# Attention's step regrouped, and the mLSTM in pairs of heads, in a hybrid layer's inference step

## The chip, the cores and the metric

The kernel runs on one core of one Trainium2 chip. The metric is the device time of one execution in microseconds; the number for a kernel is the median of its runs. PE is TensorE, DVE is VectorE, ACT is ScalarE, POOL is GpSimd, SP is the engine that issues most DMAs. Everything is fp32.

## The reference, cut to what matters

One inference step of a two-layer encoder for a prompt of 2048 tokens and a sample of 64 tokens with a past of 1024. Layer 0 projects its input into two parallel mixers, whose results are gated, joined and projected. Layer 1 is a gated DeltaNet and is not touched here. The first mixer is attention over 8 heads (96 wide for scores, 64 wide for values), causal in chunks of 64:

```python
s = einsum('bqhd,bkhd->bhqk', q, k) * (q.shape[-1] ** -0.5)
p = softmax(where(mask, s, -inf), axis=-1)
o = einsum('bhqk,bkhd->bqhd', p, v)
```

The second is the mLSTM over 4 heads (64 wide for q and k, 128 wide for v), with a state C, a normaliser n and a running maximum m:

```python
sqk = einsum('bhlk,bhsk->bhls', q, k) * exp(dmat - m[..., None])
num = w_inter[..., None] * einsum('bhlk,bhkv->bhlv', q, C0) + einsum('bhls,bhsv->bhlv', sqk, v)
den = w_inter * einsum('bhlk,bhk->bhl', q, n0) + sum(sqk, axis=-1)
h   = num / maximum(abs(den), exp(-m))[..., None]
C1  = decay_end[..., None, None] * C0 + einsum('bhl,bhlk,bhlv->bhkv', wk, k, v)
n1  = decay_end[..., None] * n0 + einsum('bhl,bhlk->bhk', wk, k)
```

## The kernel before, in words

The program is a chain of phases: `setup`, `project_a`, `attend`, `mlstm`, `project_c`, `local`, `recur`. Each phase ends with all engines meeting. Inside a phase every engine has its own stream, written by hand, and the streams meet by semaphores.

**`attend`.** The order of tiles is the sample tile (64 queries, 1088 keys: 9 key tiles, the last of 64) and then prompt tiles 0 to 15 of 128 queries; prompt tile t has t + 1 key tiles of 128. A step `s` is one head of one tile, 8 x 17 = 136 steps and 5 to drain. PE's loop (end of its block) does in step s: `scores(s)` (L974, one matmul per 512 keys), then the work of older heads: `turn(s - 1, g)` (L987) transposes the probabilities of the head before, in groups of up to 4 key tiles, and `values(p, js)` (L1009) multiplies transposed probabilities by v for a pair of older heads, one head into PSUM partitions 0 to 63 and the other into 64 to 127, in turn. Half of the pair's key tiles are done in each step. Before the change they are cut into as many portions as there are groups, and a portion follows each group of transposes. An fp32 matmul leaves two records in the trace, a transpose one.

The scores stand in PSUM (`ps`, 16 key tiles wide). A tile of more than 8 key tiles has two pieces (halves of `ps`), so the scores of a piece wait (`before_at`) until the exp of the same piece of the head before has read it. A tile of up to 8 has one piece, and heads alternate between the halves. DVE adds the diagonal mask (L1185), takes the row maximum of each piece (L1191, L1188, L1195), and then copies those transposed groups whose running number is even (`copies(s - 1, 0)`, L1075) out of the two PSUM buffers `pst`. ACT does the exp (L1109, one ACTIVATE and an accumulator read for each piece) and copies the odd groups (L1082): before the change the first of its copies goes ahead of the exp of piece 0 and the second ahead of the exp of piece 1. The transposes of a group wait for the copy of the group two before it. Once in a tile, at step 8k + 12, PE transposes the finished output back (L1021), DVE divides and gates it (L1205 to L1215), and POOL stores it (L949).

Between these, `gates(s)` does the mLSTM's gate sums and exponents, and POOL sets the initial mLSTM state at the start: a memset, and three DMAs for the sample's maximum, C and n.

**`mlstm`.** 17 tiles (16 prompt tiles, then the sample). Per tile, PE runs `numerators(t)` (for each of the 4 heads: L1430, intra: sq by v, 128 rows; and at once L1431, inter: qwT by C, 64 rows, into the same PSUM), `updates(t)` (L1441, kw by v, into PSUM partitions 0 to 63 of the banks CA and CB), `maxima(t + 1)` (L1378), `scores(t + 1)` (L1387, 64 rows), `turn_qk(t + 2)` (L1369), `turn_qw(t + 1)` (L1395), then the output projection of the tile before (`project`, L1415, 16 matmuls of 512 columns), and `turn_mix(t)` (L1406). ACT's `split_heads` (L1472, L1473) copies the transposed q, k and qw, which come with two heads on 128 partitions, into tiles of 64 partitions for all heads. DVE's `heads`, `mask`, `gated`, `state` (L1591, L1595), `weigh` (L1543) and `residual` follow. `BANK` and `order` name the PSUM bank of each product and the order in which a bank's products follow each other. SP loads q, k, v two to three tiles ahead and stores the two states at the end (`store_state`, 3 DMAs each).

Of the kernel before, what the change touches and what calls it, by code (L numbers as in the profile page):

```python
# [777 lines left out]
def attend(nc, io, sc, K):  # L778


    with ExitStack() as ctx:
# [142 lines left out]
        def _(pool):  # L924
# [29 lines left out]
            pool.wait_ge(m_init_in, 48)  # L954

        @block.tensor
        def _(pe):
# [90 lines left out]
            for s in STEPS:  # L1048
# [31 lines left out]
        def _(act):  # L1080
# [13 lines left out]
            for s in STEPS:  # L1094
                gates(s)
                mine = copies(s - 1, 1) if 1 <= s <= N else []
                for i in range(2):
                    if i < len(mine):
                        copy_turned(act, copy, s - 1, mine[i])
                    if s < N and i < pieces[head(s)[0]]:  # L1100
                        t, h = head(s)
                        n = rows(t)
                        if i == 0:
                            act.wait_ge(row_max, s + 1)
                            if s >= 2:
# [5 lines left out]
                                             accum_out=sums[at(t) % 2][:n, h, i:i + 1]).then_inc(expd, 1)  # L1111
                k = (s - 11) // H
# [8 lines left out]
        def _(dve):  # L1121
# [3 lines left out]
            def gates(s):  # L1125
# [20 lines left out]
                if s == 26:  # L1146
# [10 lines left out]
                    dve.wait_ge(m_init_in, 48)  # L1157
# [60 lines left out]
def mlstm(nc, io, sc, K):  # L1218


    with ExitStack() as ctx:
# [3 lines left out]
        def sem(name):  # L1225
# [17 lines left out]
        qT = sb("qT", [MK, MH, P])  # L1243
        kT = sb("kT", [MK, MH, P])
        qwT = sb("qwT", [MK, MH, P])
# [13 lines left out]
        x1_stored = [sem(f"x1_stored{u}") for u in range(2)]  # L1259
        qkv_in = [sem(f"qkv_in{u}") for u in range(RING)]  # L1260
# [4 lines left out]
        BANK = {"numA": 0, "qwT": 0, "numB": 1, "mixT0": 1, "CA": 2, "CB": 3, "y0": 4, "turn": 5, "y1": 5, "D": 6, "mixT1": 6,  # L1265
                "qk": 7}
        order = [(n, 0) for n in ("turn", "qk", "D")] + [("turn", 1), ("qwT", 0)]
        for t in range(TILES + 1):
            now, behind, ahead = t < TILES, t > 0, t + 1 < TILES
            order += [(n, t) for n in ("numA", "numB", "CA", "CB") if now]  # L1270
            order += [(n, t + 1) for n in ("D", "qk") if ahead]
# [30 lines left out]

        block = ctx.enter_context(nc.Block())

        @block.sync
        def _(sp):
# [12 lines left out]
            def store_state(s):  # L1319
                pre, last = "ps"[s], (NT - 1, TS)[s]  # L1320
                for name in ("CA", "CB"):
                    used(sp, name, last)
# [1705 lines left out]
```

## Time and profile before

| | us |
|---|---|
| median of 3 runs | 3954.46 (3951.67 to 3955.92) |
| the profiled execution's own time | 3945.66 |
| its span, first to last instruction | 3944.1 |
| PE busy | 3713.9, 94% of the span, mean granted clock 0.958 |
| PE's weight loads / DVE / ACT / POOL busy | 2163.4 / 1693.4 / 1090.2 / 402.7 |
| PE busy in `attend`'s scores, transposes, values (L974, L987, L1009) | 303.6, 197.9, 203.6 |
| PE busy in `mlstm`'s projection (L1415) | 236.5 |

The busy time of PE is the union of matmuls that overlap, and the end of each is modelled; times from one start to the next are the better measure of what a matmul costs. Most of the kernel's time lies in phases that the change doesn't touch. The profiled execution is one of the faster ones, so its span is a little below the median.

### The profile page before, as it was taken

Reading aid. Unit: us, or ns where it says so; the run is one execution under the profiler, and the core shown is the slowest. Engines: PE = TensorE matmul, PEld = TensorE weight load, DVE = VectorE, ACT = ScalarE, POOL = GpSimd, SP = SyncE. Lnnn points to the kernel's source line nnn. Section 1 sums busy time; section 2 is a strip of 40 time slices with the busy share of each in tenths; the row PEclk is TensorE's granted clock in tenths of the full one; section 3 lists DMA queues with packets and bytes.
Section 4 is the critical chain, followed back from the end, with each engine's and each line's share of the span. In section 5 each row is a group of like instructions: output and inputs, shape, how many; then the busy total and the mean of one; then the engine's idle time right before and its main releaser. Section 6 shows DMA issues by size and latency. Waiting matters only on the chain. (4 is left out here: it accounts for less than half of the span.)

```text
span 3944.1 us, 46043 instructions
## 1 busy us (share of the span) xinstructions
PE 3713.9 (94%) x17237; PEld 2163.4 (55%) x17237; DVE 1693.4 (43%) x2959; ACT 1090.2 (28%) x2809; POOL 402.7 (10%) x553
## 2 busy tenths in 40 slices
PE   7899999999979999998999499999999989699998
PEld 3455555555445555665555355555555558666665
DVE  2122222222235555554544244344443447477784
ACT  0211121121124444432211223233232236322222
POOL 0000000000000000000000010000000001343451
PEclk9899999999959999998999699999999998799999
DMA  5712221221073000004321611111111129855652
GB/s 179 241 60 63 78 66 53 75 72 58 28 180 77 25 23 19 11 9 142 107 86 59 221 43 47 53 60 55 44 59 39 55 82 259 235 156 157 173 146 80
DMA packets 349425, 362.15 MB, mean 92 GB/s; under 512 B 129539, under 2 KB 277742, under 8 KB 347054
## 3 DMA queue, kind: packets, MB, share of 16 engines
q1 hardware_dynamic: 307238, 305.44, 26.1%
q10 hardware_dynamic: 35112, 30.37, 2.5%
q0 software_dynamic: 6880, 23.73, 2.1%
q8 instruction: 124, 2.03, 0.2%
q14 instruction: 71, 0.58, 0.0%
HBM read 231.45 MB, written 128.01 MB: 91 GB/s over the span
## 5 line engine op out<-in xcount | busy, mean ns | idle before, releaser
L523 PE MATMUL a_bank<-a_w_in,a_hT 128*128 128x512 f32 (+4 forms) x1904 | 754.1, 554 | 2.2 <-ACT a_hT L612 2.2
L1849 PE MATMUL d_bank<-d_hT,d_w_in 128*128 128x512 f32 (+1 forms) x1920 | 724.0, 534 | 8.1 <-DMA d_w_in<-in_c_w_in 4.5
L523 PEld LDWEIGHTS a_bank<-a_w_in,a_hT 128*128 128x128 f32 (+1 forms) x1904 | 351.5, 187 | 367.5 <-issue 316.6
L1849 PEld LDWEIGHTS d_bank<-d_hT,d_w_in 128*128 128x128 f32 x1920 | 339.7, 195 | 351.1 <-issue 338.2
L974 PE MATMUL c_ps<-c_kT,c_q 96*128 96x512 f32 (+5 forms) x688 | 303.6, 576 | 23.2 <-DMA c_kT<-scratch_kT 15.9
L2670 PE MATMUL r_bank<-k_w_next,r_mixT 128*128 128x512 f32 (+1 forms) x544 | 250.3, 610 | 2.1 <-ACT r_mixT L2728 2.1
L1855 PE MATMUL d_bank<-d_w_in,d_hT 128*128 128x344 f32 (+3 forms) x816 | 245.2, 455 | 0.0
L1982 DVE SCALAR_TENSOR_TENSOR d_cv<-d_xb,k_wconv,d_cv 128x512 f32<-128x512 f32 (+1 forms) x360 | 236.9, 658 | 12.8
L1415 PE MATMUL m_bank<-m_w_out,m_mixT 128*128 128x512 f32 (+1 forms) x544 | 236.5, 593 | 0.7 <-ACT m_mixT L1499 0.7
L1980 DVE TENSOR_SCALAR d_cv<-d_xb,k_wconv 128x512 f32<-128x512 f32 (+1 forms) x120 | 52.9, 441 | 396.7 <-ACT d_xb L1922 389.3
L1191 DVE TENSOR_REDUCE c_part<-c_ps 128x1 f32<-128x1024 f32 (+9 forms) x144 | 137.6, 960 | 178.9 <-PE c_ps L974 176.5
L974 PEld LDWEIGHTS c_ps<-c_kT,c_q 96*128 96x128 f32 (+1 forms) x688 | 124.0, 197 | 158.0 <-issue 133.1
L987 PE MATMUL c_pst<-k_consts,c_prob 128*128 128x128 f32 (+1 forms) x1160 | 197.9, 287 | 13.1 <-ACT c_prob L1109 7.4
L1009 PE MATMUL c_pso<-c_probT,c_v 128*64 128x128 f32 (+1 forms) x2320 | 203.6, 291 | 0.2 <-DVE c_probT L1075 0.2
L1109 ACT ACTIVATE c_prob<-c_ps,c_negmax 128x1024 f32<-128x1024 f32 (+8 forms) x208 | 176.9, 852 | 81.1 <-DVE c_negmax L1195 43.1
L1855 PEld LDWEIGHTS d_bank<-d_w_in,d_hT 128*128 128x128 f32 (+1 forms) x816 | 149.8, 187 | 81.2 <-issue 11.3
L1082 ACT ACTIVATE c_probT<-c_pst 128x512 f32<-128x512 f32 (+3 forms) x172 | 94.2, 547 | 313.3 <-PE c_pst L987 313.0
L987 PEld LDWEIGHTS c_pst<-k_consts,c_prob 128*128 128x128 f32 (+1 forms) x1160 | 132.4, 145 | 81.0 <-issue 46.8
L1415 PEld LDWEIGHTS m_bank<-m_w_out,m_mixT 128*128 128x128 f32 (+1 forms) x544 | 100.3, 187 | 124.6 <-issue 124.5
L2670 PEld LDWEIGHTS r_bank<-k_w_next,r_mixT 128*128 128x128 f32 (+1 forms) x544 | 99.3, 189 | 116.7 <-issue 112.2
L1925 ACT ACTIVATE d_xb<-d_cv 128x512 f32<-128x512 f32 (+1 forms) x120 | 66.6, 555 | 337.0 <-DVE d_cv L1982 337.0
L1922 ACT ACTIVATE d_xb<-d_bank 128x512 f32<-128x512 f32 (+1 forms) x120 | 62.7, 522 | 343.2 <-PE d_bank L1849 335.6
(364 smaller groups left out, 4408.1 us busy)
## 6 DMA issues: line engine op xcount, KB each, us to landing
k_n_kv<-scratch_qkv SPq DMA_DIRECT2D x17, 1024.0 KB, 5.3
scratch_qkv<-d_ts SPq DMA_DIRECT2D x64, 256.0 KB, 2.3
a_w_ada<-in_c_w_ada SPq DMA_DIRECT2D x16, 768.0 KB
d_w_in<-in_c_w_in ACTq DMA_DIRECT2D x6, 2048.0 KB, 21.3
l_kT<-scratch_g_kT SPq DMA_DIRECT2D x17, 512.0 KB, 5.4
l_qT<-scratch_g_qT SPq DMA_DIRECT2D x17, 512.0 KB, 5.7
k_n_kT<-scratch_g_kT SPq DMA_DIRECT2D x17, 512.0 KB, 5.8
r_qT<-scratch_g_qT SPq DMA_DIRECT2D x17, 512.0 KB, 8.3
```

Of the source, the lines that this page charges most:

```text
L523: mm = nc.tensor.matmul(o[:n, 0:w], hT[u][:, k, :n], w_in[:, k, c0:c0 + w], start=(k == 0), stop=(k == KD - 1))
L974: mm = nc.tensor.matmul(ps[:n, o:o + b - a], q[k % 2][:, h, :n], kT[:, h, col0[t] + a:col0[t] + b], start=True, stop=True)
L987: mm = nc.tensor.transpose(pst[c % 2][:w, j % 4, :n], prob[s % 2][:n, j * P:j * P + w], ident[:n, :n])
L1009: mm = nc.tensor.matmul(pso[k % 2][u * DV:(u + 1) * DV, h0 // 2, :n], v[:w, col0[t] // P + j, (h0 + u) * DV:(h0 + u + 1) * DV], probT[(2 * ...
L1082: return nc.scalar.activation(out, src, ACT.Copy)
L1109: nc.scalar.activation(prob[s % 2][:n, c0:c1], ps[:n, o:o + c1 - c0], ACT.Exp, bias=negmax[:n, s % 2:s % 2 + 1], accum_out=sums[at(t) % 2] ...
L1191: nc.vector.tensor_reduce(part[:n, s % 2, i:i + 1], ps[:n, o:o + c1 - c0], AXX, ALU.max).then_inc(part_max, 1)
L1415: mm = nc.tensor.matmul(o[:n, :], mixT[:, k, :n], w_out[:, k, half * 512:(half + 1) * 512], start=(k == 0), stop=(k == KD - 1))
L1849: mm = nc.tensor.matmul(o[:, 0:w.w], w_in[:, k, w.a * P:(w.a + 1) * P], hT[w.r % 2][:, k, 0:w.w], start=(k == 0), stop=(k == KD - 1))
L1855: mm = nc.tensor.matmul(o[:n, 0:c1 - c0], hT[w.r % 2][:, k, w.a * P:w.a * P + n], w_in[:, k, GC + c0:GC + c1], start=(k == 0), stop=(k == ...
L1982: ins = nc.vector.scalar_tensor_tensor(cv[:, 0:w.w], xb[u][:, j:j + w.w], tap[j], cv[:, 0:w.w], ALU.mult, ALU.add)
L2670: mm = nc.tensor.matmul(o[:n, :], mixT[:, k, :n], w_out[:, k, half * 512:(half + 1) * 512], start=(k == 0), stop=(k == KD - 1))
```

## The change

In `attend`, PE does the first two groups of transposes, then all of the step's values, and then the remaining groups. ACT makes its copy of group 0 or 1 ahead of the exps and those of groups 2 and 3 behind both exps.

In `mlstm`, heads 2a and 2a + 1 lie at partitions 0 to 63 and 64 to 127 of one tile (`place(h)`): q, k, qw and the states C. PSUM banks hold even heads (`num0`, `qk0`) and odd heads (`num1`, `qk1`). The numerators are done as four intra products and then four inter products, the inter ones alternating between the two partition halves; the next tile's scores move ahead of the updates and alternate too; the updates write both PSUM halves of one bank. ACT's copies and DVE's state additions are merged over the 128 partitions, DVE's weigh and decay are split in two. The initial state takes 5 DMAs on POOL in place of 3, the stores of the states 10 on SP in place of 6. The diff, cut to its core:

```diff
@@ attend, gpsimd
-                pool.dma_start(K["m_C1"][:, :, 0:MV], io["state_mlstm_C"].rearrange("h k v -> k h v")).then_inc(m_init_in, 16)
-                pool.dma_start(K["m_C1"][:, :, MV:], io["state_mlstm_n"].rearrange("h k -> k h").unsqueeze(2)).then_inc(m_init_in, 16)
+                for b in range(2):
+                    half = slice(b * MK, (b + 1) * MK)
+                    pool.dma_start(K["m_C1"][half, :, 0:MV], io["state_mlstm_C"].rearrange("(a b) k v -> b k a v", b=2)[b]).then_inc(m_init_in, 16)
+                    pool.dma_start(K["m_C1"][half, :, MV:], io["state_mlstm_n"].rearrange("(a b) k -> b k a", b=2)[b].unsqueeze(2)).then_inc(m_init_in, 16)
@@ attend, tensor
-                    for g in range(n_g):
+                    for g in range(min(2, n_g)):
                         turn(e, g)
-                        values(p, js[g * len(js) // n_g:(g + 1) * len(js) // n_g])
+                    if js:
+                        values(p, js)
+                    for g in range(2, n_g):
+                        turn(e, g)
@@ attend, scalar
+                if mine and mine[0] < 2:
+                    copy_turned(act, copy, s - 1, mine[0])
                 for i in range(2):
-                    if i < len(mine):
-                        copy_turned(act, copy, s - 1, mine[i])
...
+                for g in mine:
+                    if g >= 2:
+                        copy_turned(act, copy, s - 1, g)
@@ mlstm
-        BANK = {"numA": 0, "qwT": 0, "numB": 1, "mixT0": 1, "CA": 2, "CB": 3, "y0": 4, "turn": 5, "y1": 5, "D": 6, "mixT1": 6,
-                "qk": 7}
+        BANK = {"num0": 0, "qwT": 0, "num1": 1, "mixT0": 1, "C": 2, "qk1": 3, "y0": 4, "turn": 5, "y1": 5, "D": 6, "mixT1": 6,
+                "qk0": 7}
+        def place(h):
+            return slice(h % 2 * MK, h % 2 * MK + MK), h // 2
@@ mlstm, tensor: scores
+                banks = [claim(pe, f"qk{b}", t) for b in range(2)]
                 used(pe, "turn", t)
                 for h in range(MH):
-                    mm = nc.tensor.matmul(o[:n, h * P:h * P + n], kT[:, h, :n], qT[:, h, :n], start=True, stop=True)
+                    (half, a), (o, fill) = place(h), banks[h % 2]
+                    mm = nc.tensor.matmul(o[:n, a * P:a * P + n], kT[half, a, :n], qT[half, a, :n], start=True, stop=True)
@@ mlstm, tensor: numerators
-                for half, name in enumerate(("numA", "numB")):
-                    o, fill = claim(pe, name, t)
-                    for h in range(2):
-                        c = slice(h * (MV + 1), (h + 1) * (MV + 1))
-                        nc.tensor.matmul(o[:n, c], sq[:n, 2 * half + h, :n], vx[u][:n, 2 * half + h, :], start=True, stop=False)
-                        mm = nc.tensor.matmul(o[:n, c], qwT[:, 2 * half + h, :n], C[s][:, 2 * half + h, :], start=False, stop=True)
-                    mm.then_inc(fill, 1)
+                for h in range(MH):
+                    a, o = h // 2, banks[h % 2][0]
+                    mm = nc.tensor.matmul(o[:n, a * (MV + 1):(a + 1) * (MV + 1)], sq[:n, h, :n], vx[u][:n, h, :],
+                                          start=(a == 0), stop=False)
...
+                used(pe, "qwT", t)
+                if 0 < t < TS:
+                    used(pe, "C", t - 1)
+                for h in range(MH):
+                    (half, a), (o, fill) = place(h), banks[h % 2]
+                    mm = nc.tensor.matmul(o[:n, a * (MV + 1):(a + 1) * (MV + 1)], qwT[half, a, :n], C[s][half, a, :],
+                                          start=False, stop=(a == 1))
@@ mlstm, tensor: updates
-                        mm = nc.tensor.matmul(o[0:MK, c], kw[t % 2][:n, 2 * half + h, :], vx[u][:n, 2 * half + h, :],
-                                              start=True, stop=True)
+                    half, a = place(h)
+                    mm = nc.tensor.matmul(o[half, a * (MV + 1):(a + 1) * (MV + 1)], kw[t % 2][:n, h, :], vx[u][:n, h, :],
+                                          start=True, stop=True)
@@ mlstm, tensor: the loop
                 numerators(t)
+                if t + 1 < TILES:
+                    scores(t + 1)
                 updates(t)
                 if t + 1 < TILES:
                     maxima(t + 1)
-                    scores(t + 1)
@@ mlstm, scalar
-                split_heads(qT, o[:, 0:2 * P], rows(t))
-                split_heads(kT, o[:, 2 * P:], rows(t), MK ** -0.5).then_inc(free, 1)
+                nc.scalar.activation(qT[:, :, :n], by_head(o[:, 0:2 * P], n), ACT.Copy)
+                nc.scalar.activation(kT[:, :, :n], by_head(o[:, 2 * P:], n), ACT.Copy, scale=MK ** -0.5).then_inc(free, 1)
@@ mlstm, vector: state
-                for half, name in enumerate(("CA", "CB")):
-                    o, free = take(dve, name, t)
-                    nc.vector.tensor_tensor(C[s][:, 2 * half:2 * half + 2, :], C[s][:, 2 * half:2 * half + 2, :],
-                                            o[0:MK, 0:2 * (MV + 1)].rearrange("p (h v) -> p h v", v=MV + 1), ALU.add).then_inc(free, 1)
-                    used(dve, name, t)
+                o, free = take(dve, "C", t)
+                nc.vector.tensor_tensor(C[s][:, :, :], C[s][:, :, :], values_of(o, P), ALU.add).then_inc(free, 1)
+                used(dve, "C", t)
```

For the sample's last tile a semaphore is added between the intra and the inter products.

## Rows read from the trace of the kernel before

**Rows 1.** The page, part 1: busy time, share and instructions of each engine.

```profile
PE 3713.9 (94%) x17237; PEld 2163.4 (55%) x17237; DVE 1693.4 (43%) x2959; ACT 1090.2 (28%) x2809; POOL 402.7 (10%) x553
```

**Rows 2.** Windows: length, busy time of PE, PEld, DVE, ACT, POOL; PEclk, DMA share, GB/s.

```profile
1100.00:1168.00 68.00, 58.56 (x288) 31.12 (x286) 20.74 (x55) 20.75 (x59) 0.00 (x0) 0.53 0.74 178
...
1411.00:1457.00 46.00, 44.80 (x302) 26.75 (x301) 24.97 (x49) 19.97 (x45) 1.07 (x2) 1.00 0.09 21
...
1830.00:2120.00 290.00, 290.00 (x1171) 170.24 (x1169) 143.63 (x311) 59.54 (x158) 13.10 (x13) 1.00 0.30 96
```

**Rows 3.** Timeline of PE, a step with 16 key tiles: start us, length us, instruction.

```profile
1706.81 3.70 PE L974 MATMUL c_ps<-c_kT,c_q 96*128 96x512 f32 x8
...
1710.35 0.60 PE L987 MATMUL c_pst<-k_consts,c_prob 128*128 128x128 f32 x4
...
1710.88 0.66 PE L1009 MATMUL c_pso<-c_probT,c_v 128*64 128x128 f32 x8
...
1711.47 0.66 PE L987 MATMUL c_pst<-k_consts,c_prob 128*128 128x128 f32 x4
...
1714.99 3.70 PE L974 MATMUL c_ps<-c_kT,c_q 96*128 96x512 f32 x8
```

**Rows 4.** Timeline of DVE and ACT in the same step.

```profile
1710.88 1.22 DVE L1191 TENSOR_REDUCE c_part<-c_ps 128x1 f32<-128x1024 f32 x1
...
1712.33 1.11 ACT L1109 ACTIVATE c_prob<-c_ps,c_negmax 128x1024 f32<-128x1024 f32 x1 [0.74 <-DVE c_negmax L1195]
...
1713.34 0.19 ACT L1109 ACTIVATION_READ_ACCUMULATOR c_prob<-c_ps,c_negmax 128x1 f32 x1
```

**Rows 5.** Timeline of a step with 10 key tiles.

```profile
1421.07 2.42 PE L974 MATMUL c_ps<-c_kT,c_q 96*128 96x512 f32 x6
...
1423.32 0.60 PE L987 MATMUL c_pst<-k_consts,c_prob 128*128 128x128 f32 x4
...
1425.20 1.12 ACT L1109 ACTIVATE c_prob<-c_ps,c_negmax 128x1024 f32<-128x1024 f32 x1 [0.65 <-DVE c_negmax L1195]
```

**Rows 6.** Timeline of POOL: stores of prompt tiles 6, 7, 10, 11 and 14.

```profile
1328.44 0.54 POOL L949 DMA_DIRECT2D scratch_mix<-c_o  x1 [30.69 <-DVE c_o L1215]
...
1367.10 0.54 POOL L949 DMA_DIRECT2D scratch_mix<-c_o  x1 [37.59 <-DVE c_o L1215]
...
1507.04 0.54 POOL L949 DMA_DIRECT2D scratch_mix<-c_o  x1 [48.04 <-DVE c_o L1215]
...
1559.50 0.55 POOL L949 DMA_DIRECT2D scratch_mix<-c_o  x1 [51.38 <-DVE c_o L1215]
...
1742.02 0.54 POOL L949 DMA_DIRECT2D scratch_mix<-c_o  x1 [63.21 <-DVE c_o L1215]
```

**Rows 7.** Timeline of PE in one mLSTM tile, up to the next tile's numerators.

```profile
1962.32 0.39 PE L1430 MATMUL m_bank<-k_m_vx,m_sq 128*128 128x129 f32 x2
1962.64 0.49 PE L1431 MATMUL m_bank<-k_m_C,m_qwT 64*128 64x129 f32 x2
...
1965.56 1.10 PE L1441 MATMUL m_bank<-k_m_vx,m_kw 128*64 128x129 f32 x8
1966.59 1.16 PE L1378 MATMUL m_bank<-k_m_Mr,k_m_negI 68*128 68x128 f32 x8
1967.68 1.16 PE L1387 MATMUL m_bank<-m_qT,m_kT 64*128 64x128 f32 x8
...
1969.47 13.90 PE L1415 MATMUL m_bank<-m_w_out,m_mixT 128*128 128x512 f32 x32
...
1984.08 0.39 PE L1430 MATMUL m_bank<-k_m_vx,m_sq 128*128 128x129 f32 x2
```

**Rows 8.** Timeline of DVE in the same mLSTM tile.

```profile
1973.33 0.69 DVE L1543 TENSOR_TENSOR m_sq<-m_bank,m_e 128x512 f32<-128x512 f32 x1
```

**Rows 9.** Timeline of PE at attention's end: value products alone.

```profile
1769.44 3.71 PE L1009 MATMUL c_pso<-c_probT,c_v 128*64 128x128 f32 x64 [0.20 <-DVE c_probT L1075]
```

**Rows 10.** Timeline of PE's weight loads in the phase `local`.

```profile
3268.20 1.87 PEld L2286 LDWEIGHTS l_bank<-k_consts,l_sq 128*128 128x128 f32 x16
```

More of the change, by code:

```diff
@@ L1242, in mlstm @@
         sq = sb("sq", [P, MH, P])
-        qT = sb("qT", [MK, MH, P])
-        kT = sb("kT", [MK, MH, P])
-        qwT = sb("qwT", [MK, MH, P])
+        qT, kT, qwT = (sb(n, [P, MH // 2, P]) for n in ("qT", "kT", "qwT"))
         qw, kw = ([sb(f"{n}{u}", [P, MH, MK]) for u in range(2)] for n in ("qw", "kw"))
@@ L1262, in mlstm @@
         ident, negm = (K["consts"][:, CONST_NAMES.index(n), :] for n in ("ident", "neg"))
-        BANK = {"numA": 0, "qwT": 0, "numB": 1, "mixT0": 1, "CA": 2, "CB": 3, "y0": 4, "turn": 5, "y1": 5, "D": 6, "mixT1": 6,
-                "qk": 7}
-        order = [(n, 0) for n in ("turn", "qk", "D")] + [("turn", 1), ("qwT", 0)]
+        BANK = {"num0": 0, "qwT": 0, "num1": 1, "mixT0": 1, "C": 2, "qk1": 3, "y0": 4, "turn": 5, "y1": 5, "D": 6, "mixT1": 6,
+                "qk0": 7}
+        order = [(n, 0) for n in ("turn", "qk0", "qk1", "D")] + [("turn", 1), ("qwT", 0)]
         for t in range(TILES + 1):
             now, behind, ahead = t < TILES, t > 0, t + 1 < TILES
-            order += [(n, t) for n in ("numA", "numB", "CA", "CB") if now]
-            order += [(n, t + 1) for n in ("D", "qk") if ahead]
+            order += [(n, t) for n in ("num0", "num1") if now]
+            order += [(n, t + 1) for n in ("qk0", "qk1") if ahead]
+            order += [("C", t)] if now else []
+            order += [("D", t + 1)] if ahead else []
             order += [("turn", t + 2)] if t + 2 < TILES else []
@@ L1490, in turned_qw @@
                 o, free = take(act, "qwT", t)
-                split_heads(qwT, o[:, 0:2 * P], rows(t)).then_inc(free, 1)
+                nc.scalar.activation(qwT[:, :, :rows(t)], by_head(o[:, 0:2 * P], rows(t)), ACT.Copy).then_inc(free, 1)
             def turned_mix(t):
@@ L1538, in weigh @@
                 n = rows(t)
[L1539 removed]
                 dve.wait_ge(e_ready, t + 1)
                 if t >= 1:
[L1542 to L1543 removed]
+                    done(dve, "num1", t - 1)
+                for b in range(2):
+                    o, free = take(dve, f"qk{b}", t)
+                    nc.vector.tensor_tensor(sq[:n, b:MH:2, :n], by_head(o[:n, 0:2 * P], n), e[:n, b:MH:2, :n],
+                                            ALU.mult).then_inc(free, 1)
             def residual(t, half):
@@ L1561, in heads @@
                 n = rows(t)
-                num = [take(dve, name, t) for name in ("numA", "numB")]
-                for half in range(2):
-                    o = num[half][0][:n, 0:2 * (MV + 1)].rearrange("p (h v) -> p h v", v=MV + 1)
-                    ch.link(nc.vector.tensor_copy(dn[:n, 2 * half:2 * half + 2], o[:, :, MV]))
+                num = [take(dve, f"num{b}", t) for b in range(2)]
+                for b in range(2):
+                    ch.link(nc.vector.tensor_copy(dn[:n, b:MH:2], values_of(num[b][0], n)[:, :, MV]))
                 ch.link(nc.vector.scalar_tensor_tensor(dn[:n, 0:4], dn[:n, 0:4], -1.0, dn[:n, 0:4], ALU.mult, ALU.max))
```

75 lines of the change are left out of this document (39 added, 36 removed).

## The prediction

> **What bounds the kernel now.** I read the page first: TensorE (PE) is busy 94% of the span [rows 1]. That alone says little, so I cut the span into stretches. Attention runs from about 1094 to 1776 us, the mLSTM from 1783 to 2168 us. In the mLSTM's 290 us between 1830 and 2120 PE is busy all 290.00 us at a granted clock of 1.00, the 2.4 GHz level; in tile 9 of attention it is busy 44.80 of 46.00 us [rows 2]. The change touches nothing outside these two phases, so what it is worth is what it takes from PE there, until another chain binds. "Busy" hides something, though: records are pipelined, so I read start to start.
>
> A 16-tile attention step (one head of prompt tile 15): scores at 1706.81, transposes at 1710.35, next scores at 1714.99 [rows 3], so 3.54 us of scores and 4.64 us of the rest. A 10-tile step has 2.25 us of scores [rows 5]. The difference, 1.29 us for 6 key tiles, gives 0.215 us per key tile in two records: 0.107 us per record of 128 columns, plus about 0.1 us. Four transposes should take 0.43 us, but 0.53 to 0.59 us pass before the value product starts, and 8 value records take from 1710.88 to 1711.47, 0.59 us [rows 3]. Value records go to the two column halves of the array in turn, and 64 of them in a row take 3.71 us, 0.058 us each with the drain [rows 9], so eight cost 0.43 too. Each change between transposes (128x128) and values (128x64) thus costs 0.59 - 0.43 = 0.16 us beyond the work. The same is seen in the mLSTM tile: one numerator pair takes from 1962.32 to 1962.64 and all 16 records (129 columns, 1.72 us of work) until 1965.56, 3.24 us [rows 7].
>
> **Attention: what changes.** With g groups of up to four key tiles a step now goes S T V T V ... and then T T V T T. For g = 4 that takes out 6 changes of shape beside V (3 V to T become 1, 4 T to V become 1, V to S becomes T to S, which I take at nothing since both use full width of 128 columns), for g = 3 four, for g = 2 two, for g = 1 none. PE's saving is 0.94, 0.63 and 0.31 us per step. The work is unchanged; so are all DMAs of this loop.
>
> What is late next: with two pieces the scores of the next head need the PSUM that exp of this head's first piece frees. In the 16-tile step exp starts at 1712.33 and its accumulator read runs from 1713.34 for 0.19 us [rows 4], so scores could start at about 1713.59, 3.24 us after the first transpose. PE's new rest is 4.64 - 0.94 = 3.70 us: PE still binds, by 0.46 us. The mask and the second reduce (1.22 us) [rows 4] shrink with fewer keys, but the first reduce then still runs when the scores end. In the 10-tile step exp starts at 1425.20, 1.88 us after the transposes at 1423.32 [rows 5]; adding 1.20 us and 0.06 us of hand-over gives 3.14 us, against 2.40 us of PE work. So there the chain binds. Shifting these two examples by the lengths of the reduces I get chains of 3.20, 3.13, 3.05, 2.98 us for 9, 10, 11, 12 key tiles, and below PE's rest (3.04 to 3.70) for 13 to 16.
>
> ScalarE's copy of group 2 or 3 moves behind both exps. It is needed when its PSUM buffer is refilled, in the next step, after 2 us or more of scores: that cover hides it; without it each step would cost one copy, about 0.6 us. In exchange the copy of group 2 (0.6 us) no longer sits between the two exps, and copying group 1 ahead of exp no longer waits for a value product. The transposes of groups 2 and 3 wait for the copies of 0 and 1; VectorE makes one of them only after its reduces, at about 2.0 to 2.7 us, while PE arrives there at 2.8 to 3.3 us with 16 tiles and 2.3 to 2.5 us with 9 or 10, where the chain binds anyway.
>
> Sum, with GpSimd's stores of finished tiles as milestones; each lies in the middle of the next tile [rows 6]:
> - g = 2: 32 steps by 0.31 = 10.0 us.
> - 1328 to 1367, half 8, half 9 key tiles: beyond these, 4 steps by 0.2 = 0.8.
> - 1367.10 to 1507.04: 24 steps, 5.83 us each now. New: scores 2.36 + chain 3.09 + 0.02 = 5.47, so 0.36 by 24 = 8.6.
> - 1507.04 to 1559.50: 8 steps of 6.56; new mean of 5.66 and 5.94, plus 0.05: 0.71 by 8 = 5.7.
> - 1559.50 to 1742.02: 24 steps of 7.61, by 0.94 = 22.6, and the last 4 = 3.8.
> Together 51.5 us; I take off 3.5 for the step in each tile in which VectorE also finishes the tile, and nothing for the sample tile at the start, which waits on key loads at a clock of 0.53 [rows 2] (bounds 0 and 5 us). **Attention: 48 us**, bounds 35 and 55.
>
> **mLSTM: what changes.** The period is 1984.08 - 1962.32 = 21.76 us per tile, of which 7.15 lie between the numerators and the output projection at 1969.47 [rows 7]. The work in them: numerators 1.72, updates 0.86, maxima 0.86, scores 0.86, six transposes 0.64, sum 4.94; the other 2.2 us are changes of tiling: seven inside the numerators (0.20 us each after the first), then to 128x64 for the updates, to the maxima, and to 64 rows for the scores. New order: four intra products (128 rows, 0.86), four inter products and then the next scores (both 64 rows), updates in two column halves, maxima, transposes. Three changes and the step to transposes are left, 0.7 us, so 1.5 us go. The updates alternate between column halves as the values do: 0.43 in place of 0.86. The inter products and the scores alternate between partitions 0 to 63 and 64 to 127, into different banks. No row shows two row halves at once. Bounds: nothing (0.107 us each, as every row at present), or half as the column halves have it, 0.86 us a tile less. I take the half, since the column pair of [rows 9] is the nearest case of two parts of the array used in turn. 1.5 + 0.43 + 0.86 = 2.8 us a tile, by 16 prompt tiles **45 us**; the sample tile has 64 rows throughout and saves nothing that counts.
>
> A rule speaks against the 0.43: the Trainium skill ("TensorE: Matmul & The Clock Gate", Part 3) says that a weight load overlaps matmuls in flight only where the row group differs, which the two column halves do not. By that rule the updates would save nothing, 7 us less in all. The 0.058 us of [rows 9] already disagrees.
>
> At nothing: six half-height ACT copies become three, two state additions one, one weigh two, one decay two; these are hidden behind the 13.7 us projection, sq(t+1) being started at 1973.33 and used at 1984.08 [rows 8]. If that cover were gone the weigh's extra 0.15 us would cost 2.6 us over 17 tiles. The numerators wait for the scores' weights first and for qwT only before the inter products, which can only help. Moving the scores ahead of the updates puts them in front of kw's wait; kw is long ready. VectorE's first denominator copy now waits for numerators that end some 1.6 us earlier. GpSimd gets two more DMA issues ahead of its first gate loads, which are used only when the first tile is finished; SP gets four more for the states while PE still projects the last tile. Both bounds: 0 and 3 us.
>
> **Sum.** 48 + 45 = 93 us. The profiled execution took 3945.7 us (span 3944.1); it would take 3853. The median of three is 3954.5, 8.8 above it, so I forecast 3862 for the median.
>
> **Rivals.**
> 1. Row halves don't run side by side. For: sixteen loads of 128 columns take 1.87 us, 0.117 each, though the matmuls behind them have only 8 columns [rows 10]; if loads are the limit, a 64-row record with 128 columns of weights can't go faster, while values have 64 columns. That loses 0.86 by 16 = 14 us: 3876. Against: two row halves have separate partitions, and [rows 10] is one full-height tile. On the same question, the page named above has row tiles starting 4 ns apart.
> 2. The exp chain is 0.5 us longer than I take (VectorE's reduces and copies meet in another order). Then tiles of 9 to 12 gain nothing (16 us lost) and those of 13 to 16 lose 0.37 to 0.06 a step (6 us): 3884. For: 24 steps already sit near it. Against: nothing is added ahead of the reduces.
> 3. Slower: PE idles about 1 us in each 5.5 us step of the tiles with 9 to 11 keys, and its clock falls there to the 1.2 GHz level, as in the sample tile (0.53 with 58.56 of 68 us busy) [rows 2]. Each step would carry some 4.5 us more; with 24 steps that is 108 us, 15 more than is won: 3969. It decides from about 21 such steps on. Against: those tiles already stall on this chain and show 1.00 [rows 2].
> 4. The change of shape isn't what costs the 0.16 us (but, say, the start of any new group). Then only the halved products count, 20 us or less, and with row halves serial too, nothing: 3934 to 3952.
>
> **Chances.** Forecast 0.60, rival 1 0.24, rival 2 0.10, rival 3 0.02, rival 4 0.04. The range goes from 3846 (attention 55, mLSTM 48, sample 5) to 3894 (rivals 1 and 2 nearly together). A measurement of this kernel tells about 0.2%, 8 us, from no change. Faster by more 0.95, within 0.02, slower 0.03.
>
> **What would show it.** In a 16-tile step: 3.7 us between first transpose and next scores, no wait on exp; in the 10-tile step 3.1 us and a wait on ScalarE's exp. In an mLSTM tile: period 18.9 to 19.0 us; 8 intra records 0.86, then 8 inter and 8 scores in 0.9 us (rival 1: 1.7). Clock 1.00 from 1243 us on. The forecast is wrong if 16-tile steps keep more than 4 us there, or if PE waits for a copy of transposes.

## The result, and the profile after

The changed kernel takes 3862.26 us (median of 4 runs, 3859.53 to 3865.66), the kernel before 3953.07 us (4 runs). The ratio is 0.9773, with a 95% interval of 0.9756 to 0.9790: 2.3% faster, 90.8 us by the medians. The two profiled executions differ by less, 3944.1 - 3864.1 = 80.0 us, since before's lies 7 us below its median and after's 3 us above. A later set of runs of the changed kernel gave 0.9766 (0.9753 to 0.9779).

The page of the changed kernel, its span and part 1:

```profile
span 3864.1 us, 46030 instructions
...
PE 3622.8 (94%) x17237; PEld 2138.7 (55%) x17237; DVE 1685.9 (44%) x2976; ACT 1067.2 (28%) x2758; POOL 401.0 (10%) x555
```

PE's share is still 94%, and as many matmuls ran. PE's busy time is 91 us less [rows 1]: the work is the same, only packed tighter, so the share of busy time could not have told the gain.

An attention step with 16 key tiles, in the timeline of all engines without weight loads (start us, length us, instruction, in brackets the idle time before it and what ended it):

```profile
1682.81 3.60 PE L976 MATMUL c_ps<-c_kT,c_q 96*128 96x512 f32 x8
...
1686.24 1.04 PE L989 MATMUL c_pst<-k_consts,c_prob 128*128 128x128 f32 x8
...
1687.21 1.97 PE L1011 MATMUL c_pso<-c_probT,c_v 128*64 128x128 f32 x32
...
1689.11 1.09 PE L989 MATMUL c_pst<-k_consts,c_prob 128*128 128x128 f32 x8
1689.24 0.19 ACT L1114 ACTIVATION_READ_ACCUMULATOR c_prob<-c_ps,c_negmax 128x1 f32 x1
...
1690.04 3.60 PE L976 MATMUL c_ps<-c_kT,c_q 96*128 96x512 f32 x8
```

From the first transpose to the next scores 1690.04 - 1686.24 = 3.80 us pass, where it was 4.64 with as many value records, 32 [rows 3]. Eight transposes take 0.97 and 0.93 us, the values 1.90. The scores ahead of them take 1686.24 - 1682.81 = 3.43 us, where they took 3.54: they now stand behind transposes and no longer behind values, and the price of that change of shape had been part of their time. Together the step takes 7.23 us, where it took 8.18: 0.95 us less. The accumulator read of the first exp ends 0.6 us before the scores start: the exp chain does not bind here.

A step with 10 key tiles, PE's timeline and then ACT's:

```profile
1403.53 1.04 PE L989 MATMUL c_pst<-k_consts,c_prob 128*128 128x128 f32 x8
1404.50 1.31 PE L1011 MATMUL c_pso<-c_probT,c_v 128*64 128x128 f32 x20
1405.74 0.44 PE L989 MATMUL c_pst<-k_consts,c_prob 128*128 128x128 f32 x2
1406.66 2.42 PE L976 MATMUL c_ps<-c_kT,c_q 96*128 96x512 f32 x6 [0.49 <-ACT c_prob L1114]
```

```profile
1405.41 1.11 ACT L1114 ACTIVATE c_prob<-c_ps,c_negmax 128x1024 f32<-128x1024 f32 x1 [0.64 <-DVE c_negmax L1203]
1406.42 0.19 ACT L1114 ACTIVATION_READ_ACCUMULATOR c_prob<-c_ps,c_negmax 128x1 f32 x1
```

Here PE stands for 0.49 us until ACT's exp releases the PSUM half; 1406.66 - 1403.53 = 3.13 us, and exp starts 1.88 us after the first transpose, as in [rows 5]. This is the new bound of the middle tiles.

GpSimd's stores of prompt tiles 0, 1, 6, 7, 10, 11 and 14 (the counterparts of [rows 6]):

```profile
1181.98 0.55 POOL L951 DMA_DIRECT2D scratch_mix<-c_o  x1 [16.38 <-DVE c_o L1223]
...
1208.08 0.54 POOL L951 DMA_DIRECT2D scratch_mix<-c_o  x1 [25.01 <-DVE c_o L1223]
...
1322.36 0.54 POOL L951 DMA_DIRECT2D scratch_mix<-c_o  x1 [28.09 <-DVE c_o L1223]
...
1360.19 0.55 POOL L951 DMA_DIRECT2D scratch_mix<-c_o  x1 [36.76 <-DVE c_o L1223]
...
1493.79 0.54 POOL L951 DMA_DIRECT2D scratch_mix<-c_o  x1 [44.78 <-DVE c_o L1223]
...
1540.84 0.55 POOL L951 DMA_DIRECT2D scratch_mix<-c_o  x1 [45.99 <-DVE c_o L1223]
...
1700.65 0.54 POOL L951 DMA_DIRECT2D scratch_mix<-c_o  x1 [55.62 <-DVE c_o L1223]
```

One mLSTM tile on PE, up to the next tile's numerators (the counterpart of [rows 7]):

```profile
1918.41 1.04 PE L1425 MATMUL m_bank<-k_consts,m_mix 128*128 128x128 f32 x8
1919.85 1.13 PE L1445 MATMUL m_bank<-k_m_vx,m_sq 128*128 128x129 f32 x8 [0.40 <-ACT m_mixT L1522]
1920.90 0.72 PE L1455 MATMUL m_bank<-k_m_C,m_qwT 64*128 64x129 f32 x8
1921.45 0.61 PE L1405 MATMUL m_bank<-m_qT,m_kT 64*128 64x128 f32 x8
1922.00 0.66 PE L1466 MATMUL m_bank<-k_m_vx,m_kw 128*64 128x129 f32 x8
1922.59 1.16 PE L1395 MATMUL m_bank<-k_m_Mr,k_m_negI 68*128 68x128 f32 x8
...
1924.24 13.90 PE L1434 MATMUL m_bank<-m_w_out,m_mixT 128*128 128x512 f32 x32
...
1939.41 1.13 PE L1445 MATMUL m_bank<-k_m_vx,m_sq 128*128 128x129 f32 x8 [0.40 <-ACT m_mixT L1522]
```

The period is 1939.41 - 1919.85 = 19.56 us, where it was 21.76. From numerators to projection it is 4.39 us, where it was 7.15. Inter products, scores and updates take 0.55, 0.55 and 0.59 us for 8 records. But there is a new row of idle time: PE waits 0.40 us for ACT's copy of the turned mix before every tile's numerators. The transposes ahead of it start at 1918.41, so 1.44 us pass where 8 transposes need 0.87.

**Where the 80.0 us between the two traces come from**, by milestones (phase starts, the stores above, the last projection):

| stretch | before | after | gain |
|---|---|---|---|
| start of the kernel to attention's first instruction | 1093.83 | 1093.03 | 0.8 |
| sample tile | 75.09 | 71.47 | 3.6 |
| to the store of prompt tile 2 | 54.28 | 60.92 | -6.6 |
| to tile 6 (two groups) | 105.24 | 96.94 | 8.3 |
| to tile 7 | 38.66 | 37.83 | 0.8 |
| to tile 10 (three groups, exp chain) | 139.94 | 133.60 | 6.3 |
| to tile 11 | 52.46 | 47.05 | 5.4 |
| to tile 14 (four groups) | 182.52 | 159.81 | 22.7 |
| to the mLSTM's start | 40.91 | 38.33 | 2.6 |
| mLSTM to its last projection | 370.03 | 334.76 | 35.3 |
| to the start of the projection phase's loads | 29.27 | 28.27 | 1.0 |
| all the rest | 1761.87 | 1762.09 | -0.2 |

Two rows were not foreseen: 6.6 us lost early in attention, and some 9 us missing in the mLSTM. The first rows scatter from profile to profile: over the traces of this case the sample tile takes 71.5 to 74.0 us with the new order and 74.5 and 75.1 with the old one. The experiments below take these two, the terms of the sum and the rivals.

### The profile page after: what moved, and what is told of

The parts are those of the page before. It is cut to its first block and busy times, and to the rows that moved or that the text cites. A ratio compares the mean times of both kernels' runs of the same rounds, so it can differ in the third digit from the quotient of the medians.

```text
span 3864.1 us, 46030 instructions
## 1 busy us (share of the span) xinstructions
PE 3622.8 (94%) x17237; PEld 2138.7 (55%) x17237; DVE 1685.9 (44%) x2976; ACT 1067.2 (28%) x2758; POOL 401.0 (10%) x555
## 5 line engine op out<-in xcount | busy, mean ns | idle before, releaser
L989 PE MATMUL c_pst<-k_consts,c_prob 128*128 128x128 f32 (+1 forms) x1160 | 169.9, 283 | 9.5 <-ACT c_prob L1114 5.0
L1011 PE MATMUL c_pso<-c_probT,c_v 128*64 128x128 f32 (+1 forms) x2320 | 159.3, 284 | 0.8 <-DVE c_probT L1080 0.8
```

The source lines that it names most:

```text
L989: mm = nc.tensor.transpose(pst[c % 2][:w, j % 4, :n], prob[s % 2][:n, j * P:j * P + w], ident[:n, :n])
L1011: mm = nc.tensor.matmul(pso[k % 2][u * DV:(u + 1) * DV, h0 // 2, :n], v[:w, col0[t] // P + j, (h0 + u) * DV:(h0 + u + 1) * DV], probT[(2 * ...
```

## The experiments

All are edits of the changed kernel unless it says otherwise, and ratios are to the kernel before; that of the changed kernel is 0.9773, or 0.9766 in the later set.

### The two parts apart

`attn_only` is the kernel before with attention's edits alone; `mlstm_only` the changed kernel with attention's three edits undone:

```diff
-                    for g in range(min(2, n_g)):
-                        turn(e, g)
-                    if js:
-                        values(p, js)
-                    for g in range(2, n_g):
-                        turn(e, g)
+                    for g in range(n_g):
+                        turn(e, g)
+                        values(p, js[g * len(js) // n_g:(g + 1) * len(js) // n_g])
```

> The kernel before with the attention part of the change alone. Theory: the two parts are independent and each gives what its stretch of the two traces shows: attention's steps from prompt tile 3 on give about 44 us, the sample tile 3 to 4 us, less 0 to 7 us for a wait on a load of queries in prompt tile 2; so 40 to 50 us faster than before, 3903 to 3913 us. Rival (the halved products of the mLSTM give all of the gain, a change of shape costs nothing): under 10 us faster.

> The changed kernel with attention's step put back. Theory: 35 to 36 us faster than before (the mLSTM's period goes from 21.76 to 19.58 us per tile for 16 tiles), 3917 us; with the first run of this batch the gains add up to the whole 91 us within 8 us. Rival (each part also helps or hurts the other through the clock or the DMAs): the sum is off by more than 8 us.

Measured: 3902.52 us, ratio 0.9875 (0.9859 to 0.9892), and 3909.76 us, ratio 0.9901 (0.9885 to 0.9918). By the ratios these are 49 and 39 us of that set's 3951, together 89, and the whole is 90 (0.0227 x 3951). The parts add up. `mlstm_only` came out 7 us below its expectation of 3917; its interval, 32 to 45 us, holds both the 35 of the trace and the 45 of the forecast, so here the traces have to decide. From attention's last store to the mLSTM's last projection they show 376.6 us before, 341.5 in the changed kernel and 342.3 in `mlstm_only`: 34 to 35 us. In attention, the stretch from the store of tile 2 to that of tile 14 takes 518.8 us in both traces with the old order on PE and 475.2 to 475.3 in every trace with the change's order: 43.6 us with hardly any scatter. Rival 4, with 20 us at most from halved products alone, falls: attention's products are the same as before and give 49 us.

### What a change of shape costs in attention

```diff
                     if js:
-                        values(p, js)
+                        values(p, js[:len(js) // 2] if n_g > 2 else js)
                     for g in range(2, n_g):
                         turn(e, g)
+                        if g == 2:
+                            values(p, js[len(js) // 2:])
```

> The changed kernel with attention's values cut into two portions where a step has three or four groups: T T V T V T. That puts back two changes of shape a step and no work. Theory (0.157 us for each change): a step of 13 to 16 key tiles takes 0.31 us longer, 32 steps, 10 us; in those of 9 to 12 the exp chain covers most of it (0 to 3 us); so 10 to 13 us slower than the changed kernel, 0.980 to 0.981 of before. Rival (what was saved was not the changes but the waits for copies, or the start of groups of transposes, whose number stays): within 2 us.

Measured: 3877.34 us, ratio 0.9814 (0.9797 to 0.9830), 16 us slower than the changed kernel. PE's timeline of a step with 16 key tiles:

```profile
1690.87 1.04 PE L989 MATMUL c_pst<-k_consts,c_prob 128*128 128x128 f32 x8
1691.84 1.09 PE L1011 MATMUL c_pso<-c_probT,c_v 128*64 128x128 f32 x16
1692.87 0.66 PE L989 MATMUL c_pst<-k_consts,c_prob 128*128 128x128 f32 x4
1693.45 1.09 PE L1011 MATMUL c_pso<-c_probT,c_v 128*64 128x128 f32 x16
1694.48 0.66 PE L989 MATMUL c_pst<-k_consts,c_prob 128*128 128x128 f32 x4
1694.97 3.60 PE L976 MATMUL c_ps<-c_kT,c_q 96*128 96x512 f32 x8
```

No idle time stands in it. It takes 1694.97 - 1690.87 = 4.10 us up to the scores, 0.30 more than the 3.80 of the changed kernel, with the same 16 transposes and 32 value records. Sixteen value records take 1.03 us where 0.86 are work, four transposes 0.58 where 0.43 are. From the stores of tile 11 to 14 it takes 167.0 us in place of 159.8: 7.2 us over 24 steps, 0.30 a step for two changes, 0.15 us each. The term of the sum is right. Where I took the exp chain to cover the change, it did not: tiles 7 to 10 take 138.8 in place of 133.6 us (0.22 a step), tiles 10 to 11 50.4 in place of 47.05 (0.42 a step). That is why it is 16 and not 10 to 13 us. What in those steps meets the chain I did not isolate.

### ScalarE's copies where they were

```diff
-                if mine and mine[0] < 2:
-                    copy_turned(act, copy, s - 1, mine[0])
                 for i in range(2):
+                    if i < len(mine):
+                        copy_turned(act, copy, s - 1, mine[i])
...
-                for g in mine:
-                    if g >= 2:
-                        copy_turned(act, copy, s - 1, g)
```

> The changed kernel with ScalarE's copies where they were: one ahead of each exp. Theory: with the new order on PE the second copy (group 2 of the head before) waits for transposes that come behind the values, so the second exp starts some 0.5 to 1 us later, but it is needed only when the second half of the next scores begins, 1.7 us after their start; the exp chain of the first piece does not change; within 4 us of the changed kernel. Rival (the second exp becomes the chain, since nothing of the next head's second piece can start): tiles with 9 to 12 key tiles take 0.5 us longer a step, 15 us slower or more.

Measured: 3859.10 us, ratio 0.9766 (0.9750 to 0.9782), the same as the changed kernel. The intervals between stores agree with it within 0.1 us from tile 2 on. This part of the change does nothing that shows: the gain in attention is the order on PE alone, and the second piece's exp has enough slack to start later.

### The gap ahead of the numerators

```diff
-        BANK = {"num0": 0, "qwT": 0, "num1": 1, "mixT0": 1, "C": 2, "qk1": 3, "y0": 4, ...
+        BANK = {"num0": 0, "qwT": 0, "num1": 1, "mixT0": 4, "C": 2, "qk1": 3, "y0": 4, ...
```

> The changed kernel with the first half of the turned mix in the PSUM bank of y0 (bank 4) in place of num1's (bank 1). Theory: the 0.57 us that PE idles in every tile between the transposes of the mix and the numerators is the wait for ScalarE's copy of bank 1, since both numerator banks are now claimed ahead of the first product. Then 8 transposes take 0.87 us up to the numerators, the period falls from 19.58 to 19.01 us and the kernel by 16 x 0.57 = 9 us, to about 3853. Rival (PE waits there for something else, such as VectorE's weighed scores or the claim of bank 0): the gap stays, no change.

Measured: 3852.64 us, ratio 0.9752 (0.9735 to 0.9768), 8.3 us faster than the changed kernel by the ratios, 5.5 by its ratio in the later set. The intervals overlap, so the trace has to settle it. PE's timeline of one tile:

```profile
1927.87 1.04 PE L1425 MATMUL m_bank<-k_consts,m_mix 128*128 128x128 f32 x8
1928.74 1.06 PE L1445 MATMUL m_bank<-k_m_vx,m_sq 128*128 128x129 f32 x8
...
1933.06 13.90 PE L1434 MATMUL m_bank<-m_w_out,m_mixT 128*128 128x512 f32 x32
...
1947.67 1.06 PE L1445 MATMUL m_bank<-k_m_vx,m_sq 128*128 128x129 f32 x8
```

The wait is gone, 0.87 us lie between transposes and numerators, and the period is 1947.67 - 1928.74 = 18.93 us, 0.63 less than the changed kernel's. From attention's last store to the mLSTM's last projection it takes 330.8 us in place of 341.5. So the gap was bank 1: the transposes of the mix and the odd heads' numerators share it, and the new numerators claim both their banks ahead of the first product. Before the change they claimed bank 0 first and came to bank 1 only 1.6 us later, at about 1963.9 us in the tile of [rows 7]. By then both of ScalarE's copies (two records in one row) were done:

```profile
1962.14 1.08 ACT L1499 ACTIVATE m_mixT<-m_bank 128x512 f32<-128x512 f32 x2 [10.50 <-PE m_bank L1406]
```

### Do the halves have to alternate?

```diff
-                for h in range(MH):
+                for h in (0, 2, 1, 3):
```

in `scores`, the inter products and `updates`.

> The changed kernel with the heads of the mLSTM's scores, inter products and updates taken in the order 0, 2, 1, 3, so that the two halves of the array alternate only once. Theory: 0.43 us per group come from two halves at work at once, for which neighbours must differ in their half; with two of four matmuls behind one of the same half each group of 8 records takes about 0.7 us (three of four neighbours serial: 6 or 7 of 8 record times of 0.107 us), so +0.3 us for each of three groups, 0.9 us per tile, 14 to 16 us slower than the changed kernel (0.9815 of before). Bounds 0.25 to 0.43 us a group. Rival (the products are faster for another reason, such as only half of the rows or columns being loaded or stored): no change. Rival for the updates alone (a weight load overlaps only where the row group differs, so their column halves never overlapped): the scores and inter products get slower, the updates stay at 0.59 us.

Measured: 3864.21 us, ratio 0.9783 (0.9767 to 0.9800). Expected were 14 to 16 us more; by the ratios it is 4 us slower than the changed kernel, or 7 by its ratio in the later set. PE's timeline:

```profile
1941.69 0.72 PE L1455 MATMUL m_bank<-k_m_C,m_qwT 64*128 64x129 f32 x8
1942.24 0.71 PE L1405 MATMUL m_bank<-m_qT,m_kT 64*128 64x128 f32 x8
1942.89 0.67 PE L1466 MATMUL m_bank<-k_m_vx,m_kw 128*64 128x129 f32 x8
1943.49 1.16 PE L1395 MATMUL m_bank<-k_m_Mr,k_m_negI 68*128 68x128 f32 x8
```

The inter products take 0.55 us as before, the updates 0.60 for 0.59, the scores 0.65 for 0.55. So the order within a group of 8 records hardly counts, as long as each half gets four of them: the second half's records start while the first half's are at work. The first 0.05 us of the scores show it, `same_half` first and then the kernel before, 0.15 us behind the start of its scores:

```profile
1942.24 0.38 PE L1405 MATMUL m_bank<-m_qT,m_kT 64*128 64x128 f32 x2
...
1967.68 0.37 PE L1387 MATMUL m_bank<-m_qT,m_kT 64*128 64x128 f32 x1
```

Two score records are under way at once where one half alone has one. What counts is seen against the kernel before, whose 8 score records have the same shape, all use the same half and take 1.08 us [rows 7]. So the run came out as its first rival says (no change), but not for that rival's reason: no less is loaded or stored than before. Rival 1 of the prediction (row halves can't run side by side, because the loads of weights limit them) is out: at 0.107 us a load it would take 0.86 us or more. The rival for the updates is out too, though its sign came (the updates stay as they were): they took 1.03 us in one column half [rows 7] and take 0.59 in two.

### The numerators head by head, with and without the gap

```diff
+                used(pe, "qwT", t)
+                if 0 < t < TS:
+                    used(pe, "C", t - 1)
                 for h in range(MH):
                     a, o = h // 2, banks[h % 2][0]
                     mm = nc.tensor.matmul(... sq[:n, h, :n], vx[u][:n, h, :], start=(a == 0), stop=False)
-                if t == TS:
-                    mm.then_inc(last_intra, 1)
-                    pe.wait_ge(last_intra, 1)
-                used(pe, "qwT", t)
-                if 0 < t < TS:
-                    used(pe, "C", t - 1)
-                for h in range(MH):
+                    if t == TS:
+                        mm.then_inc(last_intra, 1)
+                        pe.wait_ge(last_intra, h + 1)
                     (half, a), (o, fill) = place(h), banks[h % 2]
```

`pairwise` has this alone, `pair_bank` has the turned mix's bank changed as well.

> The changed kernel with the numerators of each head as before: intra and at once inter, so seven changes of the array's rows where there was one, and no two inter products side by side. Theory: the numerators take 3.2 us again in place of 1.6 (0.2 us for each of six changes and 0.43 for the halving), the period rises from 19.58 by 1.6 us less the 0.57 us if the wait for bank 1 is passed in the meantime, which it is not, since both banks are still claimed first: 16 x 1.6 = 26 us slower, 0.984 of before. Rival (only the halving counts, changes are free): 7 us slower.

> The numerators head by head (intra, at once inter) as in pairwise, with the turned mix's first half in bank 4, so that PE has no idle time ahead of the numerators. Theory: pairwise was 50 us slower than the changed kernel where 26 were expected because PE's short idle time in each tile, together with the sparser records behind it, let the granted clock fall in some of the tiles (0.93 to 0.94 in three stretches of 50 us). Without the idle time the clock stays at 1.00 and only the changes of shape count: period 18.93 + 1.35 = 20.3 us, 16 x 1.35 = 22 us slower than mix_bank, 3875 us (0.981). Rival (the sparse numerators alone bring the clock down): 0.93 to 0.97 in the mLSTM's stretches and 3885 us or more.

Measured: `pairwise` 3911.21 us, ratio 0.9901 (0.9885 to 0.9918): 50 us slower than the changed kernel, not 26. `pair_bank` 3880.45 us, ratio 0.9814 (0.9798 to 0.9831): 24 us slower than `mix_bank` by the ratios, as the changes of shape would have it. Windows of `pairwise` (length, busy time of PE, PEld, DVE, ACT, POOL; PEclk, DMA share, GB/s):

```profile
1900.00:1950.00 50.00, 48.73 (x212) 29.37 (x211) 24.78 (x59) 6.35 (x18) 2.72 (x3) 0.94 0.37 120
```

and of `pair_bank`:

```profile
1900.00:1950.00 50.00, 50.00 (x202) 27.82 (x200) 23.40 (x52) 6.84 (x20) 2.02 (x2) 1.00 0.27 84
```

In `pairwise` the granted clock falls to the 1.2 GHz level in some tiles: three of the windows of 50 us between 1800 and 2050 show 0.93 or 0.94. PE's timeline of such a tile, with the projections around it:

```profile
1926.27 13.90 PE L1434 MATMUL m_bank<-m_w_out,m_mixT 128*128 128x512 f32 x32
...
1941.69 0.46 PE L1448 MATMUL m_bank<-k_m_vx,m_sq 128*128 128x129 f32 x2 [0.65 <-ACT m_mixT L1521]
...
1946.37 1.13 PE L1465 MATMUL m_bank<-k_m_vx,m_kw 128*64 128x129 f32 x8
1947.43 2.08 PE L1395 MATMUL m_bank<-k_m_Mr,k_m_negI 68*128 68x128 f32 x8
...
1950.58 13.75 PE L1434 MATMUL m_bank<-m_w_out,m_mixT 128*128 128x512 f32 x31
```

The numerators start at full clock behind 0.65 us of idle time. Further on in the same tile the records take twice as long: 1.06 us from updates to maxima in place of 0.59, and from projection to projection it is 24.31 us, where the tile before has 21.39. Three such tiles, and some 0.3 us more in the tile behind each, make 9 to 10 us in this trace. The tiles at full clock, 21.39 us against 19.57, make 1.82 x 16 = 29 us, 3 more than expected, because the idle time has grown too: from transposes to numerators it is 1941.69 - 1940.01 = 1.68 us, where the changed kernel has 1.44. Together that is 38 to 39 us, against 36.5 between the spans of the two traces. This execution, at 3902.22 us, is the fastest of the four; that the 21 us which the median has beyond the 29 are the clock's as well is not shown.

With the idle time gone and the same order of products, the clock stays at 1.00 and the period is 20.53 us, 1.60 more than `mix_bank`'s 18.93; by 16 that is 25.6 us. So the sparse numerators alone don't bring the clock down, and the changed kernel's gap with dense numerators (1.00 from 1800 to 2050 us) doesn't either. The two together did, in some tiles. But the idle time is 0.65 us there and 0.40 in the changed kernel, and no run has 0.65 us with dense numerators: that the longer gap alone would do it is not excluded.

### The wait for queries

In the changed kernel's timeline of all engines, at prompt tile 2:

```profile
1190.21 1.65 PE L976 MATMUL c_ps<-c_kT,c_q 96*128 96x384 f32 x2 [4.61 <-DMA c_q<-scratch_qT]
```

PE waits 4.61 us for queries, and then one head's scores take 1.65 us busy at the low clock where they take 0.91 at full clock. The load stands behind two groups of keys and values that SP issues when the sample tile is done.

```diff
-                if k == 2:
+                if k == 5:
                     sp.wait_ge(o_full, 1)
                     load_group(2)
                     load_group(3)
```

> The changed kernel with the loads of key and value groups 2 and 3 (5 MB, first used by prompt tile 8) issued after the queries of order 5 in place of ahead of those of order 3. Theory: in prompt tile 2 PE waits 4.6 us for queries that stand behind this burst, and its clock falls to 1.2 GHz for some steps after; without the burst ahead the wait is under 1 us, and the interval between the stores of prompt tiles 0 and 1 falls from 26.1 to 19 us or less: 5 to 8 us faster, about 3855. Rival (the wait is chance in the speed of the DMAs, as before's trace has only 0.5 us of it): within 3 us of the changed kernel on the median, while its profile may show either.

Measured: 3856.57 us, ratio 0.9764 (0.9748 to 0.9780), 3.6 us below the changed kernel by the ratios, whose intervals overlap, and under 1 us by its ratio in the later set. Stores of prompt tiles 0 and 1:

```profile
1182.05 0.55 POOL L951 DMA_DIRECT2D scratch_mix<-c_o  x1 [16.38 <-DVE c_o L1223]
1200.76 0.55 POOL L951 DMA_DIRECT2D scratch_mix<-c_o  x1 [17.62 <-DVE c_o L1223]
```

The interval is 18.7 us, where the changed kernel's is 26.1; `best`, the other profile with this edit, has 18.8. But with the order unedited it differs from profile to profile: 19.5 (before), 26.1, 24.2 (`mix_bank`), 23.5 (`mlstm_only`, with attention's old order), and 19.9 in the changed kernel's second profile. Two things go into it, and the wait for queries is only one. `mlstm_only` never waits for queries between these two stores (PE's longest wait there is 0.6 us, for ScalarE's exp), and still needs 23.5 us, because the granted clock stays low. Windows from store to store, `mlstm_only` and then `q_first`:

```profile
1182.89:1206.36 23.47, 22.91 (x90) 12.85 (x90) 13.29 (x41) 7.47 (x22) 1.09 (x2) 0.56 0.26 56
...
1182.05:1200.76 18.71, 15.61 (x88) 8.80 (x87) 13.19 (x41) 7.33 (x22) 1.08 (x2) 0.91 0.21 50
```

The same stretch of `pair_bank` has no wait for queries either, 23.5 us and a clock of 0.55. So the queries do stand behind the burst, and the changed kernel's 26.1 us are a wait of 4.6 us with steps at the low clock behind it; why the clock comes back earlier in one profile than in another stays open. Nothing shows any of it to be an effect of the change. The worth of the edit on the median is not clear of the measurement.

### Both edits together

> The changed kernel with both edits: the turned mix's first half in bank 4, and the loads of groups 2 and 3 issued after the queries of order 5. Theory: the first takes 0.65 us from each of 16 mLSTM tiles (period 18.93 us), the second the wait for queries in prompt tile 2 with the steps at the low clock behind it; they lie in different phases, so they add: 9 to 10 us and 3 to 7 us, 3846 to 3850 us, 0.974 of before. Rival (the second is chance): as mix_bank alone, 3853.

> The changed kernel itself, unedited, as the measure for its two neighbours in this batch: 0.976 to 0.978 of before, 3860 to 3864 us.

Measured, in one set: `best` 3849.32 us, ratio 0.9744 (0.9731 to 0.9758), the unedited changed kernel 3858.50 us, ratio 0.9766 (0.9753 to 0.9779). Both edits give 9 us, and the bank alone, with 0.63 us less in each of 16 tiles, would account for 10; a sum of two effects is not shown. This is the fastest version, 2.6% below the kernel before.

## Why the prediction was right, point by point

**The number** (3862, measured 3862.26) is closer than its terms, and that is luck. The forecast gain was 93 us; the medians give 90.8, but the profiled execution was to take 3853 us and took 3865.66, and between the traces the gain is 80.0. The parts by themselves measure 49 and 39 us; the rows of the table give 43.1 for attention and 35.3 for the mLSTM.

**Attention, 48 us forecast.** Right, and right in its steps. A four-group step with 16 key tiles was to lose 0.94 us and loses 0.95. It keeps 3.80 us between first transpose and next scores where 3.70 were forecast, and the scores take 0.11 us less. The 24 steps with four groups were to give 22.6 us and gave 22.7. The 8 steps from tile 10 to 11 were to give 5.7 and gave 5.4; the 10-tile step's chain was to be 3.14 us and is 3.13. Three terms came out smaller: the chain-bound steps 6.3 for 8.6, the steps with two groups (with the stretch to tile 7) 9.1 for 10.8, the last stretch 2.6 for 3.8. Over all these stretches it is 46.1 us, for 51.5 less the 3.5 taken off. The sample tile, taken at nothing, shows 3.6, of which part is scatter, and the 6.6 us lost early are set against it. Rival 2 (a longer chain) is out by the same rows.

**mLSTM, 45 us forecast, 35 in the trace.** The products came as forecast: numerators to projection 4.39 us (forecast 4.35, a saving of 2.8; measured 2.76), both halves at work at once. The step that failed is the one given at nothing: "The numerators wait for the scores' weights first and for qwT only before the inter products, which can only help." I looked at the waits for data that moved, and not at the claims of banks, which moved too: the claim of bank 1 went ahead of the first product. It costs 0.57 us in each of 16 tiles, 9 us, and `mix_bank` gets it back in the trace; its period of 18.93 us is the forecast's 18.9 to 19.0.

**Rival 1** (row halves one after the other): out, 0.55 us for 8 records. The rule of the Trainium skill ("TensorE: Matmul & The Clock Gate", Part 3) that a weight load overlaps matmuls in flight only where the row group differs would have left the updates at the 1.03 us of [rows 7]. They take 0.59 in two column halves, so the trace disagrees.

**Rival 3** (the clock falls in the middle tiles of attention): out; they idle on the chain (0.49 us in the step shown), PE is busy for 131.30 us of the 140 from 1360 to 1500, and the clock stays at 1.00. A fall of the clock behind short idle times does occur in this kernel, in `pairwise`, in another place: 9 to 10 us in its trace. **Rival 4:** out by `attn_only` and `two_portions`.

**What was hidden** stayed hidden: in the mLSTM tile shown PE waits for nothing but the turned mix, so neither the decay in two parts nor the two weighs show, and with the four extra stores of the states the stretch behind the last projection takes 28.27 us, where it took 29.27.

## What to carry to other kernels

Sort small matmuls by the part of the array that they use: here each change of tiling cost 0.15 to 0.20 us, where four transposes cost 0.43, and it shows only in start-to-start times, never as idle time. It is part of the time of the group behind it, so compare whole steps with equally many records. When an order is merged, list the claims of buffers that move with it and not only the waits for data: a bank claimed ahead of the first product cost a tenth of this change's gain. A short idle time ahead of sparse matmuls can cost more than its length, because the clock may follow.

## What the runs showed of the hardware that I had not expected

- Two halves of the array work side by side without strict alternation: with four records for one half and then four for the other, 8 inter records took 0.55 us and 8 score records 0.65 us, against 1.08 us where all eight used the same half. (The two row halves wrote to different PSUM banks.)
- The granted clock fell to the 1.2 GHz level for part of a stretch in which PE was busy for 48.73 of 50 us, when 0.65 us of idle time and seven changes of the array's rows came together (`pairwise`). With those changes and no idle time (`pair_bank`), and with 0.40 us of idle time and one change (the changed kernel), it stayed at 2.4 GHz.
